# Memory rows by token tile, and a first unit that begins with one k-tile

## The reference

```
mkv = rmsnorm(mem, g_mem) @ w_mem_kv      # (256 x 1024) @ (1024 x 1024)
mk, mv = split(mkv, 2)                    # two halves of 512 columns
```

## Time and profile before

| what | value |
|---|---|
| median of three runs | 1142.04 us (1142.02 to 1142.12) |
| profiled execution: time, span | 1141.86 us, 1140.0 us |
| TensorE busy | 1130.2 us (99%), 5299 matmuls |
| VectorE busy | 656.9 us (58%) |
| ACT busy | 622.5 us (55%) |
| POOL busy | 180.9 us (16%) |
| DMA moved | 204.57 MB, mean 179 GB/s |

### The profile page before, as it was taken

How to read it: one execution, slowest core, us unless ns; L and a number is a source line. 1 busy time by engine, 2 the same in 40 slices (tenths; PEclk the granted TensorE clock), 3 DMA queues, 4 the chain that set the end, 5 groups by cost and what they waited for, 6 DMA issues and landing times.

```text
span 1140.0 us, 14044 instructions
## 1 busy us (share of the span) xinstructions
PE 1130.2 (99%) x5299; PEld 935.3 (82%) x5299; DVE 656.9 (58%) x680; ACT 622.5 (55%) x786; POOL 180.9 (16%) x123
## 2 busy tenths in 40 slices
PE   8999999999999999999999999999999999999998
PEld 7788888888888888888778888888888888888886
DVE  5735668675655544784348565454465776744442
ACT  6655556654867643644478374443355546655331
POOL 1423500000434310000032021110015100211000
PEclk9999999999999999999999999999999999999999
DMA  9644344554554554655335456445545324655530
GB/s 354 237 154 164 131 166 156 194 185 185 185 190 179 192 190 171 231 221 194 139 120 194 150 212 223 176 180 189 198 186 206 128 110 166 221 184 182 184 114 37
DMA packets 30322, 204.57 MB, mean 179 GB/s; under 512 B 3584, under 2 KB 3744, under 8 KB 6592
## 3 DMA queue, kind: packets, MB, share of 16 engines
q1 hardware_dynamic: 28752, 198.75, 48.3%
q0 software_dynamic: 1520, 5.12, 1.4%
HBM read 202.81 MB, written 1.05 MB: 179 GB/s over the span
## 4 chain that ended last, share of the span: by engine, by line
PE 94%; POOL 1%; issue 1%; DVE 1%; ACT 1%; DMA 1%; SPq 0%; DVEq 0%; POOLq 0%; ACTq 0%
PE ps L654 84%; PE aux L726 3%; PE aux L1163 1%; PE ps L776 1%; PE aux L939 1%; PE aux L925 1%; DMA mrows<-in_mem 1%; POOL sc L498 0%; PE aux L1093 0%; PE aux L1044 0%; DVE Wl L1794 0%; ACT Wh L1267 0%; POOL sq L514 0%; DVE sc L1866 0%; ACT prob L1444 0%
## 5 line engine op out<-in xcount | busy, mean ns | idle before, releaser
L1794 DVE TENSOR_TENSOR Wl<-raw,Wh 128x2048 fp32r<-128x2048 f32 x184 | 427.6, 2330 | 326.6 <-ACT Wh L1267 326.3
L654 PE MATMUL ps<-Wh,xT 128*128 128x512 f32 x1920 | 608.2, 393 | 0.0
L1267 ACT ACTIVATE Wh<-raw 128x2048 fp32r<-128x2048 f32 x184 | 349.9, 1907 | 266.5 <-PE ps L654 265.6
L654 PEld LDWEIGHTS ps<-Wh,xT 128*128 128x128 f32 x1920 | 360.5, 188 | 75.1 <-issue 1.2
L654 PE MATMUL ps<-Wl,xT 128*128 128x512 f32 x960 | 373.7, 389 | 0.0
L654 PEld LDWEIGHTS ps<-Wl,xT 128*128 128x128 f32 x960 | 180.4, 188 | 36.4 <-issue 0.5
L654 PE MATMUL ps<-Wh,hTh 128*128 128x512 f32 x256 | 100.1, 391 | 0.0
L654 PE MATMUL ps<-Wh,hTl 128*128 128x512 f32 x256 | 99.7, 389 | 0.0
L654 PE MATMUL ps<-Wl,hTh 128*128 128x512 f32 x256 | 99.6, 389 | 0.0
L654 PEld LDWEIGHTS ps<-Wh,hTl 128*128 128x128 f32 x256 | 48.0, 188 | 10.0
L654 PEld LDWEIGHTS ps<-Wl,hTh 128*128 128x128 f32 x256 | 48.1, 188 | 9.9
(11 more groups left out here) (347 smaller groups left out, 1219.2 us busy)
## 6 DMA issues: line engine op xcount, KB each, us to landing
raw<-in_wstream SPq DMA_DIRECT2D x185, 1024.0 KB, 4.7
grow<-in_post_gains POOLq DMA_DIRECT2D x4, 512.0 KB, 5.5
grow<-in_b_gate POOLq DMA_DIRECT2D x6, 256.0 KB, 3.5
mrows<-in_mem SPq DMA_DIRECT2D x2, 512.0 KB, 5.1
raw<-in_wstream SPq DMA_DIRECT2D x2, 512.0 KB, 6.4
x<-in_x SPq DMA_DIRECT2D x1, 1024.0 KB, 13.3
out<-x SPq DMA_DIRECT2D x4, 256.0 KB, 2.0
rdm<-in_ret_decays POOLq DMA_DIRECT2D x1, 768.0 KB, 6.9
```

Of the source, the lines that this page charges most:

```text
L654: mm = nc.tensor.matmul(ps[2 * pair + t][:, :], a[:, kt, t * P:(t + 1) * P], w[:, slot, j, :], start=(first and j == 0 and q == 0), stop=( ...
L1267: nc.scalar.activation(Wh[:, slot, 0:nk, :], raw[:, slot, 0:nk, :], ACT.Copy).then_inc(hi_ready, 1)
L1794: nc.vector.tensor_tensor(Wl[:, slot, 0:nk, :], raw[:, slot, 0:nk, :], Wh[:, slot, 0:nk, :].bitcast(F32), ALU.subtract).then_inc(lo_ready, 1)
```

## The change

1. The memory is loaded by token tile (`mrows[:, 0, :]`, then `mrows[:, 1, :]`) and no longer by halves of columns. Token tile 0 comes first, token tile 1 behind granule 0.
2. Granule 0 is loaded in three pieces: k-tile 0, k-tile 1, k-tiles 2 and 3; granule 1 in two. `split_part` follows these pieces.
3. The two small tables are issued from ACT's queue, ahead of its table load, and not from SP's. The rest of `cst` is issued behind granule 3.
4. The memory is transposed in five groups (`MEM_BLOCKS`): tile 0 with k-tiles 0 and 1, tile 0 with 2 and 3, tile 1 with 0 to 3, tile 0 with 4 to 7, tile 1 with 4 to 7. The copies and remainders of the memory are of 128x128 blocks, not 128x256. The fifth group takes `aux` bank 0 a second time.
5. TensorE turns groups 0 and 1, multiplies k-tiles 0 to 2 by tile 0, turns groups 2 and 3, multiplies k-tile 3 by tile 0, then k-tile 0 by tile 1, turns group 4, and multiplies k-tiles 1 to 3 by tile 1. Granule 1 goes by halves, tile 0 before tile 1 in each.
6. The warm tile is 256 wide; 14 and later 4 warm matmuls of 256 columns stand in place of 9, 6 and 2 of 512. The wait ahead of the transposes of `x` is dropped.

```diff
@@ -134,7 +134,7 @@
             used[bank] += 1
             plan[(name, first + b)] = (bank, used[bank])
-    use("memT", [0, 1, 2, 3])
+    use("memT", [0, 1, 2, 3, 0])
     use("xT", [0, 1, 2, 3])
     use("small", [0])
     use("rows20", [1])
@@ -369,7 +369,7 @@
         hrow = at("hrow", [P, 2, 2, C], R + 64)
         junk = at("junk", [P, D], R + 72)
         junk2 = at("junk2", [P, D], R + 44)
-        warm = at("warm", [P, C], R + 64, F32R)
+        warm = at("warm", [P, TOK], R + 64, F32R)
         yg = at("yg", [P, 2, D], R + 64)
         ygr = at("ygr", [P, 2, D], R + 48)
@@ -429,6 +429,9 @@
         block = ctx.enter_context(nc.Block())
+        MEM_BLOCKS = [(0, (0, 1)), (0, (2, 3)), (1, (0, 1, 2, 3)), (0, (4, 5, 6, 7)), (1, (4, 5, 6, 7))]
+        MEM_BANK = {(t, kt): b for b, (t, kts) in enumerate(MEM_BLOCKS) for kt in kts}
         def wait_unit(eng, name, t):
             if t == 0:
@@ -464,17 +467,17 @@
         @block.sync
         def _(sp):
-            sp.dma_start(gains[:, :], gpack).then_inc(sem("gains_in"), 16)
-            sp.dma_start(cst[:, 0:P], cpack[:, 0:P]).then_inc(sem("ident_in"), 16)
-            sp.dma_start(mrows[:, :, 0:C], mem_rows[:, :, 0:C]).then_inc(sem("mem_in0"), 16)
-            sp.dma_start(raw[:, 0, 0:2, :], wstream[0, :, 0:2, :]).then_inc(sem("first_in"), 16)
-            sp.dma_start(mrows[:, :, C:D], mem_rows[:, :, C:D]).then_inc(sem("mem_in1"), 16)
+            sp.dma_start(mrows[:, 0, :], mem_rows[:, 0, :]).then_inc(sem("mem_in0"), 16)
+            sp.dma_start(raw[:, 0, 0:1, :], wstream[0, :, 0:1, :]).then_inc(sem("first_in0"), 16)
+            sp.dma_start(raw[:, 0, 1:2, :], wstream[0, :, 1:2, :]).then_inc(sem("first_in1"), 16)
             sp.dma_start(raw[:, 0, 2:4, :], wstream[0, :, 2:4, :]).then_inc(landed[0], 16)
-            sp.dma_start(raw[:, 1, :, :], wstream[1]).then_inc(landed[1], 16)
+            sp.dma_start(mrows[:, 1, :], mem_rows[:, 1, :]).then_inc(sem("mem_in1"), 16)
+            sp.dma_start(raw[:, 1, 0:2, :], wstream[1, :, 0:2, :]).then_inc(sem("second_in"), 16)
+            sp.dma_start(raw[:, 1, 2:4, :], wstream[1, :, 2:4, :]).then_inc(landed[1], 16)
             sp.dma_start(raw[:, 2, :, :], wstream[2]).then_inc(landed[2], 16)
             sp.dma_start(x[:, :, :], x_rows).then_inc(sem("x_in"), 16)
+            sp.dma_start(raw[:, 3, :, :], wstream[3]).then_inc(landed[3], 16)
             sp.dma_start(cst[:, P:], cpack[:, P:]).then_inc(sem("cst_in"), 16)
-            sp.dma_start(raw[:, 3, :, :], wstream[3]).then_inc(landed[3], 16)
             by_ring = wstream[0:NG // RING * RING].rearrange("(i j) p k c -> i j p k c", j=RING)
             with sp.Fori(1, NG // RING) as i:
                 for j in range(RING):
@@ -759,39 +762,54 @@
             def keep_warm(count):
                 for _ in range(count):
-                    nc.tensor.matmul(bank("mv", 0), warm[:, 0:P], warm[:, :], start=True, stop=True)
-            def first_unit():
-                for g in range(2):
-                    for half in range(2):
-                        if half == 0:
-                            pe.wait_ge(sem("lo_half"), g + 1)
-                        else:
-                            pe.wait_ge(lo_ready, g + 1)
-                        wait_operand("memT", (2 * g + half,))
-                        for j in (2 * half, 2 * half + 1):
-                            for t in range(2):
-                                for q, (a, w) in enumerate(((memTh, Wh), (memTh, Wl), (memTl, Wh))):
-                                    mm = nc.tensor.matmul(bank("mk", t), a[:, 4 * g + j, t * P:(t + 1) * P], w[:, g, j, :],
-                                                          start=(g == 0 and j == 0 and q == 0), stop=(g == 1 and j == 3 and q == 2))
-                                if g == 1 and j == 3 and t == 0:
-                                    mm.then_inc(half_done, 1)
-                    mm.then_inc(gran_used, 1)
+                    nc.tensor.matmul(bank("mv", 0)[:, 0:TOK], warm[:, 0:P], warm[:, :], start=True, stop=True)
+            def first_block(kt, t):
+                wait_read(pe, "memT", MEM_BANK[(t, kt)])
+                for q, (a, w) in enumerate(((memTh, Wh), (memTh, Wl), (memTl, Wh))):
+                    mm = nc.tensor.matmul(bank("mk", t), a[:, kt, t * P:(t + 1) * P], w[:, kt // 4, kt % 4, :],
+                                          start=(kt == 0 and q == 0), stop=(kt == 7 and q == 2))
+                return mm
+            def turn_mem(b):
+                t, kts = MEM_BLOCKS[b]
+                pe.wait_ge(sem(f"mem_in{t}"), 16)
+                turn("memT", b, [(j * P, mrows[:, t, kt * P:(kt + 1) * P]) for j, kt in enumerate(kts)])
             pe.wait_ge(sem("warm_rows"), 1)
-            keep_warm(9)
+            keep_warm(14)
             pe.wait_ge(sem("ident_in"), 16)
-            for b in range(4):
-                if b == 2:
-                    keep_warm(6)
-                pe.wait_ge(sem(f"mem_in{b // 2}"), 16)
-                turn_rows("memT", mrows, b)
-            keep_warm(2)
-            first_unit()
+            turn_mem(0)
+            turn_mem(1)
+            keep_warm(4)
+            for kt in range(4):
+                if kt < 2:
+                    pe.wait_ge(sem("lo_part"), kt + 1)
+                else:
+                    pe.wait_ge(lo_ready, 1)
+                if kt == 3:
+                    turn_mem(2)
+                    turn_mem(3)
+                first_block(kt, 0)
+            for kt in range(4):
+                mm = first_block(kt, 1)
+                if kt == 0:
+                    turn_mem(4)
+            mm.then_inc(gran_used, 1)
+            for half in range(2):
+                if half == 0:
+                    pe.wait_ge(sem("lo_part"), 3)
+                else:
+                    pe.wait_ge(lo_ready, 2)
+                for t in range(2):
+                    for kt in (4 + 2 * half, 5 + 2 * half):
+                        mm = first_block(kt, t)
+                    if half == 1 and t == 0:
+                        mm.then_inc(half_done, 1)
+            mm.then_inc(gran_used, 1)
             def turn_x():
-                wait_operand("memT", (2, 3))
                 pe.wait_ge(sem("x_in"), 16)
                 for b in range(4):
                     turn_rows("xT", x, b)
@@ -1339,25 +1357,36 @@
                     square(scratch, rows_of[:, t, :], S(f"{key}_ss", t, t + 1), sem(f"{key}_ss"), t + 1)
+            nc.scalar.dma_start(gains[:, :], gpack).then_inc(sem("gains_in"), 16)
+            nc.scalar.dma_start(cst[:, 0:P], cpack[:, 0:P]).then_inc(sem("ident_in"), 16)
             nc.scalar.add_instruction(mybir.InstLoadActFuncSet(name=nc.get_next_instruction_name(), act_func_set_id=EXP_AND_LN,
                                                                engine=mybir.EngineType.Activation))
-            def split_half(g, half):
-                if g == 0 and half == 0:
-                    act.wait_ge(sem("first_in"), 16)
-                else:
-                    act.wait_ge(landed[g], 16)
-                ks = slice(2 * half, 2 * half + 2)
+            def split_part(g, kts):
+                arrived = {(0, 0): sem("first_in0"), (0, 1): sem("first_in1"), (0, 2): landed[0], (1, 0): sem("second_in"), (1, 2): landed[1]}
+                act.wait_ge(arrived[(g, kts[0])], 16)
+                ks = slice(kts[0], kts[-1] + 1)
                 nc.scalar.activation(Wh[:, g, ks, :], raw[:, g, ks, :], ACT.Copy)\
-                    .then_inc(hi_ready if half else sem("hi_half"), 1)
+                    .then_inc(hi_ready if kts[-1] == 3 else sem("hi_part"), 1)
+            def mem_high(b):
+                t, kts = MEM_BLOCKS[b]
+                o = wait_aux(act, "memT", b)
+                for j, kt in enumerate(kts):
+                    nc.scalar.activation(memTh[:, kt, t * P:(t + 1) * P], o[:, j * P:(j + 1) * P], ACT.Copy,
+                                         scale=gcol("g_mem", kt)).then_inc(sem("memT_hi"), 1)
             act.wait_ge(sem("gains_in"), 16)
-            for b in range(4):
-                high("memT", b, memTh, (2 * b, 2 * b + 1), "g_mem")
-                if b < 2:
-                    split_half(0, b)
-            split_half(1, 0)
-            split_half(1, 1)
+            mem_high(0)
+            split_part(0, (0,))
+            mem_high(1)
+            split_part(0, (1,))
+            split_part(0, (2, 3))
+            mem_high(2)
+            split_part(1, (0, 1))
+            mem_high(3)
+            mem_high(4)
+            split_part(1, (2, 3))
             split(2)
             square_sums("mem", mrows, junk[:, :])
             act.wait_ge(sem("small_in"), 64)
@@ -1885,24 +1914,38 @@
                     free(nc.vector.tensor_scalar(dst, o[:, :], scale, None, ALU.mult), name, b)
             nc.vector.memset(S("ga"), 1.0).then_inc(sem("ga_ones"), 1)
-            def split_half(g, half):
-                if half == 0:
```

(35 more changed lines are left out.)

## The result

The changed kernel takes **1145.1 us** (median of nine runs, 1145.05 to 1145.52) against 1142.11 for the kernel before (nine runs). The ratio is 1.0027, with a 95% interval of 1.0019 to 1.0035: 3.0 us slower. The forecast was 1144.4 with a range of 1142.1 to 1147.7. The profiled execution took 1145.09 with a span of 1143.1, so it stands for the median.

The account below looks back on a forecast made before the run. TensorE, busy 99% of the span, bounds the kernel. Moved transposes 1.3, idle 1.9, block (2,0) 0.5 later, less two early blocks 1.36, make 2.35; taken as +2.4 us: 1144.4, range 1142.1 to 1147.7.

Parts of the forecast that it names:

- the forecast case: Unit mk ends at 23.89 against 21.51, +2.4 us, giving 1144.4; chance 0.63, own range 1143.4 to 1145.2.
- The pause for group 2: Ahead of block (0,1): group 2's transposes, issued only behind block (2,0), leave TensorE idle 1.9 us, from 13.37 to 15.27.
- The hand-overs: Passing work between TensorE, ACT and VectorE in the first stage: 0.1 us each, 0.34 for the last with restart.
- The 0.24 of restart: TensorE restarting after a wait in the first stage: 0.24 us from weight load to matmul.
- The transposes in the stream: In unit mk, 12 memory transposes now stand between blocks, not ahead of them: 1.3 us.
- the early blocks: Blocks (0,0) and (1,0) are done by 9.5, ahead of the old start at 10.62: a gain of 1.36 us.
- The landing of k-tiles 2 and 3: Second part of granule 0 usable at 8.5 us; the same bytes were usable at 9.17 before.
- The saving of 0.65: Start of the loads: tables on ACT's queue cost about 0.37 us instead of about 1, so later bytes come 0.65 sooner.
- ACT's side costs nothing: ACT's two issues of about 0.45 us and its table load end by 3 us; its first work comes past 5.
- The rival of full rate: Early bytes come at 432 GB/s: k-tiles 2 and 3 usable at 6.4, only +0.3 us, 1142.3; chance 0.15.
- The low clock: Rival: sparse start leaves TensorE at 1.2 GHz, matmuls 0.41 apart past 11 us; +2.5 in all, 1146.9; chance 0.17.
- The edits costed at nothing elsewhere: Warm matmuls, extra SP issues, later `cst`, small loads, granule 5 and the dropped wait add no time.

Follow-up runs that it names:

- e3_turn_early: The changed kernel with group 2 transposed behind block (0,0) and group 3 behind block (1,0), not both behind block (2,0): 1143.91 us, ratio 1.0015.
- e5_warm_and_early: The changed kernel with 22 and 12 warm matmuls and groups 2 and 3 transposed behind blocks (0,0) and (1,0): 1142.19 us, ratio 1.000.
- e12_warm_early_tables_sp: e5_warm_and_early with the two small tables back on SP's queue ahead of the memory rows: 1143.7 us, ratio 1.002.
- e2_long_warm: The changed kernel with 22 and 12 narrow warm matmuls in place of 14 and 4: 1144.33 us, ratio 1.0019.
- e6_half_rows_first: e5_warm_and_early with token tile 0 loaded in two column halves, the second behind token tile 1, and group 3 turned behind block (3,0): 1142.3 us, ratio 1.0006.
- e9_quarters: e6_half_rows_first with k-tiles 2 and 3 split singly, tables first on SP's queue, memory in quarters, 18 and 14 warm matmuls: 1142.99 us, ratio 1.001.
- e1_tables_on_sp: The changed kernel with the two small tables issued again by SP, ahead of the memory rows: 1145.98 us, ratio 1.0034.

## Why the prediction was right

The direction, the place and nearly the size were right: +3.0 us, forecast +2.4. The mechanism was the one forecast. That the number came so near is partly luck, because errors of the same size cancelled, and one rival came true beside the forecast case.

- **The pause for group 2** was the central step, and it held. From the start of its transposes to block (0,1) it took 15.77 - 12.78 = 2.99 us; predicted 3.43. The hand-overs were mis-sized: 0.1 each and 0.34 for the last one with the restart, against 0.02, 0.02 and 0.04 in the chain. The 0.24 of restart was a misreading of the earlier trace rows: the weight load at 10.38 stood behind two warm matmuls that ran from 10.06 to 10.77, so it was no restart from idle; here weight load and matmul both start at 15.77. The idle time was 1.3, not 1.9. `e3_turn_early` showed that the late transposes cause it.
- **The transposes in the stream** held: 12 of them, 1.3 us with little more for restarts (8.76 us from 15.77 to the mark, predicted 8.62). `e5_warm_and_early` showed that they eat what the early blocks win.
- **The landing of k-tiles 2 and 3**, "can be used at 9.17 - 0.65 = 8.5", came out at 8.0. Other runs with the tables on ACT's queue have it at 8.1 to 8.8. The saving of 0.65 is mis-sized: the kernel before with that move alone gains 0.4 for the same bytes, the changed kernel 0.8 (`e5_warm_and_early` beside `e12_warm_early_tables_sp`). "Nothing in the reordering changes them" was too strong. But the landing was not what block (2,0) waited for.
- **"ACT's side costs nothing"** is the step that failed. The table took 4.8 us from issue to landing instead of 1.9, so token tile 0, in at 4.45, could be turned only at 6.02 and not at 4.8. From there ACT had no gap, and its copy of k-tiles 2 and 3 began at 8.87 and not at 8.5. VectorE was done at 11.19 and the weight load stood ready at 11.24, against the predicted 11.16: 0.37 late at ACT, and 0.29 of it hidden by the restart priced too high. That is the luck. The rival of full rate did not come true, with 8.0 far from its 6.4.
- **The low clock**, a rival with 0.17, came true. It cost 0.30 ahead of block (2,0), whose matmul came at 11.54 because nine matmuls stood 0.43 apart from 8.81 on, and 0.56 in it. No more came behind it, since the clock rose at about 12.8: 0.86, where I had priced it at 2.5. What bounded it is that blocks (0,0) and (1,0) ran mostly in time that was idle anyway. `e2_long_warm` took 0.69 back.
- The sum, at the mark: 0.08 (weights ready for block (2,0)) + 0.30 + 0.56 (clock) - 0.44 (hand-overs) + 0.14 (restarts) = 0.64 above the predicted 23.89, which is the measured 24.53.
- The edits costed at nothing elsewhere held: past 24 us TensorE has the one wait that it had before.

## What to carry to other kernels

When the start of a kernel is cut into smaller pieces, count what the consumer has queued behind each new wait: here four transposes, ready early but issued behind a block that waited for weights, cost more than two blocks won. Every piece of preparation that moves from ahead of the stream into it is paid in full. Keep TensorE busy through a sparse start, and check the level by the spacing of the matmuls. And price a queue move by an experiment: in the changed kernel it brought the first rows 2.3 us sooner and the later ones only what the two issues cost, and on the kernel before it cost more than it brought in 18 of 20 executions.

## What the runs showed of the hardware

- The place of two small tables (96 KB) changes the flow of the first megabyte: 272 and 237 GB/s from 2.8 to 7.0 us with them ahead on SP's queue, 323 and 262 with them on ACT's, in runs that differ in nothing else. The first 512 KB land 2.3 us sooner (4.45, 6.8), the second 512 KB 0.94 sooner (10.06, 11.00). The price is the tables' own landing, 4.8 us after issue instead of 1.9 (2.9 in `e12_warm_early_tables_sp`). The Trainium skill ("Trainium Kernel Development and Optimization", Key Constraints) says that the queues interleave on the same DMA engines and that a second issuer saves only issue time. The second 512 KB agree (0.95 of issue); for the first, 2.3 is more than that, and there the measurement decides. The reason isn't shown.
- 256 KB as the first memory transfer in place of 512 landed 3.2 us after its issue instead of 3.7, with the tables on ACT's queue (`e6_half_rows_first`), and 3.0 instead of 5.0 behind the tables on SP's (`e9_quarters` beside `e1_tables_on_sp`, which differ in more than that).
- Matmuls stayed at the 1.2 GHz level up to 12.7 us in the changed kernel, after 3.36 us of warm matmuls, 1.43 us without work and short pieces behind it. With 22 and 12 warm matmuls in place of 14 and 4 they stood 0.23 apart from the first block on.
- The granted clock of a window read 1.00 over stretches in which 512-column matmuls came 0.43 us apart; it read 0.50 only in the run in which the clock had been up once and fell.
- A profiled execution can differ from the common one: the kernel before with the tables on ACT's queue gave 1141.8 under the profile twice, and 1144.2 or more in the 18 others.
